# In all three attentions of a two-layer diffusion backbone, ScalarE takes a step's exponentials ahead of the copy of a turned block

## The reference

```python
def gqa_block(q, k, v):            # used by attention B (latent compressed) and C (grouped)
    s = jnp.einsum('bqgrd,bsgd->bgrqs', q, k).astype(jnp.float32) * scale
    p = jax.nn.softmax(s, axis=-1).astype(v.dtype)
    return jnp.einsum('bgrqs,bsge->bqgre', p, v)

def diff_block(q, k, v, lam):      # attention A: the difference of two softmaxes
    p = jax.nn.softmax(s, axis=-1)
    w = (p[:, 0] - lam * p[:, 1]).astype(v.dtype)
    return jnp.einsum('bhqs,bshe->bqhe', w, v)
```

## Time and profile before

| | |
|---|---|
| median of 3 runs | 2586.37 us |
| span of the profiled execution (the only time listed for it) | 2588.2 us |
| PE busy | 2488.6 us, 96% |
| DVE busy | 1386.0 us, 54% |
| ACT busy | 974.1 us, 38% |
| POOL busy | 410.9 us, 16% |
| chain of waits, share on PE | 86% |

### The profile page before, as it was taken

How to read it: one execution, slowest core, us unless ns; L and a number is a source line. 1 busy time by engine, 2 the same in 40 slices (tenths; PEclk the granted TensorE clock), 3 DMA queues, 4 the chain that set the end, 5 groups by cost and what they waited for, 6 DMA issues and landing times.

```text
span 2588.2 us, 42794 instructions
## 1 busy us (share of the span) xinstructions
PE 2488.6 (96%) x17115; PEld 2261.7 (87%) x17115; DVE 1386.0 (54%) x2367; ACT 974.1 (38%) x1713; POOL 410.9 (16%) x362
## 2 busy tenths in 40 slices
PE   7989999999999999999999999999999999999998
PEld 5878977798799999999977799668977999999998
DVE  4675366646754554245447843776476555433542
ACT  5453255424533433133244523454244243322332
POOL 0500022023020221022014000220320202200220
PEclk8999999999999999999999999999999999999999
DMA  7311232422032222322322022222210422222222
GB/s 239 97 33 57 65 98 93 131 87 59 21 117 76 66 65 78 85 65 69 111 89 74 17 66 72 92 82 74 78 50 18 131 66 65 77 74 78 78 61 81
DMA packets 252834, 202.80 MB, mean 78 GB/s; under 512 B 9877, under 2 KB 235911, under 8 KB 252679
## 3 DMA queue, kind: packets, MB, share of 16 engines
q1 hardware_dynamic: 245574, 197.67, 25.3%
q10 hardware_dynamic: 7104, 2.95, 0.4%
HBM read 196.50 MB, written 4.10 MB: 78 GB/s over the span
## 4 chain that ended last, share of the span: by engine, by line
PE 86%; DVE 5%; ACT 5%; issue 2%; DMA 1%; SPq 1%; POOL 0%; POOLq 0%; DVEq 0%; ACTq 0%
PE ps L1373 48%; PE ps L1395 7%; PE ps L1544 5%; PE ps L1558 4%; PE ps L1585 3%; PE ps L1358 3%; PE ps L1360 3%; PE ps L1359 3%; ACT prob L1828 2%; PE ps L1485 1%; PE ps L1442 1%; PE ps L1248 1%; PE ps L1502 1%; PE ps L1505 1%; ACT probT L1838 1%
## 5 line engine op out<-in xcount | busy, mean ns | idle before, releaser
L2050 DVE TENSOR_TENSOR wlo<-raw,whi 128x1024 fp32r<-128x1024 f32 (+4 forms) x284 | 357.5, 1259 | 433.7 <-ACT whi L1696 432.6
L1373 PE MATMUL ps<-hhi,whi 128*128 128x320 f32 x1856 | 426.1, 311 | 6.4 <-DVE wlo L2050 2.7
L1373 PE MATMUL ps<-hlo,whi 128*128 128x320 f32 x1856 | 424.7, 310 | 0.0
L1373 PE MATMUL ps<-hhi,wlo 128*128 128x320 f32 x1856 | 424.6, 310 | 0.0
L1696 ACT ACTIVATE whi<-raw 128x1024 fp32r<-128x1024 f32 (+4 forms) x284 | 277.7, 978 | 376.8 <-PE ps L1373 294.9
L1373 PEld LDWEIGHTS ps<-hhi,whi 128*128 128x128 f32 x1856 | 311.3, 189 | 8.8 <-DVE wlo L2050 4.0
L1373 PEld LDWEIGHTS ps<-hhi,wlo 128*128 128x128 f32 x1856 | 312.2, 189 | 0.0
L1373 PEld LDWEIGHTS ps<-hlo,whi 128*128 128x128 f32 x1856 | 311.9, 189 | 0.0
L2326 POOL TENSOR_TENSOR rstd<-smean,mhalf 128x4 f32<-128x4 f32 (+3 forms) x96 | 118.7, 1239 | 553.8 <-DVE smean L2100 553.0
L2124 DVE TENSOR_REDUCE negmax<-ps 128x1 f32<-128x640 f32 x192 | 151.6, 819 | 65.2 <-PE ps L1544 65.0
L1838 ACT ACTIVATE probT<-ps 128x512 f32<-128x512 f32 (+1 forms) x172 | 88.3, 514 | 247.4 <-PE ps L1558 247.4
(11 more groups left out here) (244 smaller groups left out, 4416.8 us busy)
## 6 DMA issues: line engine op xcount, KB each, us to landing
raw<-in_w_up SPq DMA_DIRECT2D x88, 512.0 KB, 4.9
raw<-in_w_in SPq DMA_DIRECT2D x40, 1024.0 KB, 5.2
raw<-in_w_ada SPq DMA_DIRECT2D x29, 1024.0 KB, 5.2
raw<-in_w_down SPq DMA_DIRECT2D x16, 768.0 KB, 4.8
raw<-in_w_down SPq DMA_DIRECT2D x16, 640.0 KB, 4.4
adaw<-in_w_ada SPq DMA_DIRECT2D x8, 1024.0 KB, 11.3
raw<-in_w_o SPq DMA_DIRECT2D x8, 1024.0 KB, 5.5
raw<-in_w_branch_a SPq DMA_DIRECT2D x4, 1024.0 KB, 5.0
```

Of the source, the lines that this page charges most:

```text
L1373: mm = pe.matmul(out, w[:, sub, c], m[:, kt, o:o + HALF], start=first and i == 0 and a == 0, stop=last and i == len(ks) - 1 and a == 2)
L2050: dve.tensor_tensor(dst(wlo), src, dst(whi).bitcast(F32), ALU.subtract).then_inc(S["lo_ready"], 1)
```

## The change

In a cycle the step `expo` of step i is written ahead of part 0 of `turnp` of step i - 1, instead of behind it.

```diff
--- before.py
+++ after.py
@@ -368,9 +368,9 @@
             if i == 0:
                 for step in left:
                     step()
-            turn_part(i - 1, 0)
             if i < len(seq):
                 add("expo", **seq[i])
+            turn_part(i - 1, 0)
             turn_part(i - 1, 1)
             if i >= 2:
                 now = prob_turns(seq[i - 1]) if i - 1 < len(seq) else []
```

## The result

The changed kernel takes **2624.9 us** (median of 4 runs, 2621.4 to 2631.8) against 2586.1 us for the kernel before, measured beside it: a ratio of 1.0153, with an interval of 1.0140 to 1.0166. The execution that was profiled is the slowest of the four, 2631.82 us with a span of 2630.0; the prediction gave 2635 for this span.

The account below looks back on a forecast made before the run. The prediction took PE to bound the kernel. Its terms, C 35.2 and B 16.2 minus gains of 1.6, 0.3 and 2.3, sum to +47.2 us: 2633.5 us from the median 2586.4, forecast 2623 to 2642, with 80% for 2620 to 2648.

Parts of the forecast that it names:

- the two hand-overs: All attentions: 0.10 us from DVE's maximum to ACT's exponential, 0.15 from ACT's copy to PE's third transposes.
- C's usual step: Attention C: third transposes start at 646.68 instead of 645.61, 1.07 us late, in 18 steps, 19.3 us.
- C's first turned step: First turned step of C in each layer: PE starts at 636.82 instead of 634.30, 2.52 us, twice, 5.0.
- C after a context step: Attention C: values take 0.66 instead of 1.31, so third transposes are 1.72 us late, four times, 6.9.
- The step without a gate: Attention C, two steps: a wait of 0.19 disappears, so the cost is 0.81 us each, 1.6.
- B's usual step: Attention B: third transposes start at 394.13 instead of 393.68, 0.45 us, nine times, 4.1.
- B without filler: Attention B: five steps without filler lose a wait of 0.19 and cost 0.19 us each, 1.0.
- half hidden: Rival, B and C: PE not really held or later waits absorb more, half of 51 us stays, 2610; 6%.
- the argument from A: Attention A: has steps of 5.3 us with as much idle time and still 0.98 of full clock.
- clock loss: Rival, B and C: extra waits lower PE's clock; ten stretches of 3.4 us make +17, 2650; 9%.
- faster: Rival, B and C: third transposes find their bank free, all 58 charges vanish, exponentials start earlier, 2577; 3%.
- no change: Rival: no change of order or need, PE's wait already satisfied by an older copy, time stays 2586; 2%.

Follow-up runs that it names:

- The kernel with the other bank: Changed kernel, but the third part of a turned block goes to bank 5 and is copied by DVE: 2592.5 us, ratio 1.0017 to the kernel before.
- the other bank with the old order: Third part in bank 5 with DVE's copy, but ACT's order as in the kernel before: 2604.8 us, ratio 1.0067 to the kernel before.
- the experiment with one wait: Changed kernel, but in an attention's first step PE waits for earlier items' copies only ahead of part 0: 2622.8 us, one run.
- the repeats of both kernels: Changed kernel and kernel before, each measured again unchanged: 2622.9 us (ratio 1.0143) and 2585.8 us (one run).
- A alone: Kernel before with the new order in attention A only, B and C as before: 2587.0 us, ratio 0.9997.
- the mixed order: Kernel before, copy behind the exponentials where under three blocks were turned, between them in B's three-block steps: 2585.7 us, ratio 0.9994; repeated 2583.3, 0.9986.

## Why the prediction was right

**The direction and the mechanism** came out as written. The third transposes' wait is 48.5 us in 60 places where about 50 in some 60 were named; A is shorter by 1.4 per layer (1.1 named); the loss is C's first and B's second. The kernel with the other bank shows that it is this wait: ACT's order stays new, the wait goes, and 33 us come back. Against the same kernel with the old order, the new one is then even 8.5 us shorter by the stages.

**The size** was 47.2 against 36.9 by the stages, and 39 or 37 by the two measurements. That is the lower end of the forecast itself (2623 to 2642), not its middle. The step that failed is the choice of the two hand-overs, "0.10 for the hand-over from DVE to ACT" and "I use 0.15" for the one from ACT to PE, 0.25 in each of 58 places. Measured, they are 0.04 and 0.05: in C's usual step the first maximum ends 2.20 after the scores and the exponential starts at 2.24, and the copy ends at 4.39 and PE starts at 4.44. That is 0.16 less per place, nearly the lower bound of the prediction (0.03 and 0.05), which gave 37 us. The 0.15 came from the earlier trace rows, the place in the trace of before where PE waits for a copy; but that is a first turned step, whose instruction has a second wait, and the experiment with one wait gives 0.05 there too. The trace of before could have settled it. PE's scores have one wait, for the exponentials, and the earlier trace rows have them start at 676.62. The timeline of ACT in the kernel before has what they waited for:

```profile
675.68 0.80 ACT L1828 ACTIVATE prob<-ps,negmax 128x640 f32<-128x640 f32 x1
676.35 0.21 ACT L1828 ACTIVATION_READ_ACCUMULATOR prob<-ps,negmax 128x1 f32 x1
```

The second row, the last piece of the exponential, ends at 676.56, and PE starts 0.05 to 0.06 later. The other scores that wait for ACT show the same. In the same trace ACT starts an exponential 0.03 after the maximum in 12 places where it had waited for it, and 0.09 after in 4.

**Term by term**, by the repeats of both kernels (the two hand-overs make up most of the 10.3 us by which the sum was over):

- C's usual step: 1.07 predicted, 0.90 measured (5.67 to 6.57), 18 times, the last steps among them. This is 3 of the 4.7 us that C was over.
- C's first turned step: 2.52 predicted, 2.50 measured (4.82 to 7.32). It has the two waits, so its 0.15 was right. In layer 0 there are about 1.6 us more, with the clock at half behind the wait.
- C after a context step: 1.72 predicted, 1.61 and 1.55 measured. The context step: 0.59 and 0.47. The step without a gate: 0.81 and 0.64. C in all: 34.9 and 30.2.
- B's usual step: 0.45 predicted, 0.27 measured (6.29 to 6.56), in two of nine 0.17 to 0.20. B after a context step with all its work: 1.11 and 0.93 or 1.06; the context step: 0.71 and 0.50 to 0.61; the first turned step: 1.28 and 1.20; the steps with late maxima: 1.05 and 0.93.
- B without filler was to lose 0.19 in five steps. In four it gains 0.06 to 0.08 (5.08 to 5.00): the third transposes come at 4.72, 0.18 earlier than reckoned, and the next scores follow 0.28 behind them, not 0.37. In the fifth it loses 0.05. The fourth first turned step was to lose 0.14 and gains 0.06. B after a context step without filler was a gain of 0.78, and is one of 0.85. B in all: 14.6 and 9.5.
- A: a gain of 2.3 predicted, 2.8 measured.

In B, for one, the same usual step in the timeline of the kernel after (compare):

```profile
389.70 0.82 DVE L2124 TENSOR_REDUCE negmax<-ps 128x1 f32<-128x640 f32 x1 [0.25 <-PE ps L1544]
...
390.56 0.80 ACT L1828 ACTIVATE prob<-ps,negmax 128x640 f32<-128x640 f32 x1 [0.19 <-DVE negmax L2124]
...
391.35 0.59 ACT L1838 ACTIVATE probT<-ps 128x512 f32<-128x512 f32 x1
...
391.99 0.44 PE L1558 MATMUL ps<-ident,prob 128*128 128x128 f32 x2 [0.20 <-ACT probT L1838]
```

The second maximum ends at 390.52, and from there to PE there are 0.04 + 0.79 + 0.59 + 0.05 = 1.47 us. The prediction's chain was the same with 0.10 + 0.79 + 0.60 + 0.15 = 1.64. Of the 0.17 between them 0.16 is the two hand-overs; the rest of the chain is right.

**What else in the prediction does not hold.** If each of the two hand-overs cost 0.1 more, the 58 places would cost 11.6 us more, and the upper bound would be 59 and 2645, not 53 and 2639. Half of 51 us, with the gains kept, gives 2608 for *half hidden*, not 2610. The stretch of 219.20 to 222.60 is not where PE ran one-column products: those ran from 217.02 on, ahead of it, and in the stretch PE ran transposes, values and gate products. And of attention A's five steps of 5.33 us in a layer only the first has as much idle time of PE as C's steps were to have, 1.46 us; the others have 0.42. So the argument from A against a clock loss was weaker than it was put.

**The rivals.** *Half hidden* (2610), *faster* and *no change* are out: no later wait absorbs anything in a usual step, and the transposes waited for their bank in 60 places. *Clock loss* is true to about a tenth of its 17 us. The prediction named a clock below 0.95 in B or C as a sign that it is wrong, and its profile has one: 0.92 in B at 1759.84, 3.8 us longer than in the repeat, where the clock is 1.00. The sign was badly chosen, since the kernel before has 0.95 (0.945) in its B at 1647.77 and 1.00 there in its repeat. So such falls in B come and go without the change. The prediction also said that the clock in C stays at 1.00. It does, but for 3.4 us in layer 0, in the repeat too, at a place where the kernel before has none in its two traces. Kernel after, windows: PE's wait in C's first turned step of layer 0, the stretch behind it, and the step after that:

```profile
639.00:641.00 2.00, 0.80 (x6) 0.83 (x7) 1.45 (x5) 1.41 (x4) 0.00 (x0) 1.00 0.24 70
641.20:644.50 3.30, 3.30 (x14) 2.58 (x15) 0.00 (x0) 0.44 (x1) 0.00 (x0) 0.50 0.00 0
644.60:652.00 7.40, 6.57 (x59) 4.94 (x56) 3.60 (x8) 2.53 (x6) 0.00 (x0) 1.00 0.01 2
```

PE idled 2.84 us before the transposes at 640.20; then the granted clock is 0.50, 1.2 GHz, for 3.4 us, and back at 2.4. This costs 1.57 us (101.75 against 100.18). The Trainium skill (TensorE: Matmul & The Clock Gate, section on a second failure mode, PSUM-queue depth-cycling) tells of a bfloat16 kernel in which short idles between groups of matmuls make the clock swing. This trace does not agree for the idles of 0.83 us in C's usual steps, which recur every 6.57 us at a clock of 1.00; only the one long wait is followed by a fall, and not each time. Whether the wait causes it was not tested by itself.

## What to carry to other kernels

Before an instruction is moved back in an engine's queue, ask whose buffer it frees: here a copy that ACT seemed free to take later was also the one that emptied the bank for PE's next transposes, and its slack was not ACT's to spend. A bank that is used twice in a step ties the order of the engine that empties it. When such a delay is priced, take the hand-over between engines from a row with as many waits as the instruction will have, and multiply it only then.

An order that is good for one stage need not be good for its neighbours: the same moved line gave A 1.4 us per layer and cost B 0.7 to 3.6 us in each half and C 15 in each layer. The rule that has both is to delay the copy only where no third turn follows: 4.9 us by the stages, though only 2.3 of them show in the time.

## What the runs showed of the hardware

**Low clock comes at fixed places.** Stretches at half clock, 3.4 to 23.9 us long, recur in all 14 traces near the same places of the program: its start, A's end in both layers as in the earlier trace rows, and near 830, 1320 and 2100 us. Other places have one in some traces only. The same place in the kernel after (windows):

```profile
231.50:234.50 3.00, 3.00 (x14) 3.00 (x13) 1.84 (x3) 0.00 (x0) 1.13 (x1) 0.51 0.03 7
```

How many show and how long they are differs from run to run, and the spread of a kernel's times goes with it: among 29 runs of the kernel before, 2582.0 us went with a mean granted clock of 0.991 and 2592.2 with 0.986, and a straight line through all 29 falls by 1.6 us per 0.001. The changed kernel's four runs do the same, 2621.4 at 0.990, 2624.0 at 0.988, 2625.7 at 0.987 and 2631.8 at 0.985. So a gain of 3 us in the stages, as with A alone, doesn't show in a dozen runs.

**Such a stretch follows a long wait in some traces, not surely.** In the seven traces in which PE waits about 2 us or more in C's first turned step (1.99 to 2.85), the low stretch follows in 6 of 14 layers; in the seven without that wait it follows in none of 14. Layer 0 of the changed kernel has it in both its traces, layer 1 in neither. Another place came with shorter steps: the mixed order has a stretch of 10 us at the start of B's second half of layer 0 in both its traces, where of the twelve other traces only one has one there (the other bank with the old order, 7 us). Whether the shorter steps bring it was not found out.
